# Gate and up products of a two-layer decoder trunk: seven block products in place of eight for the upper half of the input, one core

## The reference, cut to what matters

```python
D_MODEL = 1024
D_FF = 2816
...
def rmsnorm(x, g):
    xf = x.astype(jnp.float32)
    y = xf * lax.rsqrt(jnp.mean(xf * xf, axis=-1, keepdims=True) + EPS)
    return (y * g.astype(jnp.float32)).astype(x.dtype)

def swiglu(x, wi, wo):
    g, u = jnp.split(x @ wi, 2, axis=-1)
    return (jax.nn.silu(g) * u) @ wo

def ffn_half(x, g_pre, g_post, wi, wo):
    return x + 0.5 * rmsnorm(swiglu(rmsnorm(x, g_pre), wi, wo), g_post)
```

## Time and profile before

| | |
|---|---|
| runs | 2091.39 us median of 3 (2090.8 to 2091.59) |
| profiled execution, span from first to last instruction | 2089.9 us |
| PE busy | 2068.6 us, 99% |
| DVE busy | 1125.9 us, 54% |
| ACT busy | 702.9 us, 34% |
| POOL busy | 47.7 us, 2% |
| mean traffic | 97 GB/s |

### The profile page before, as it was taken

One profiled execution on the slowest core, in us unless ns is written; L12 is line 12 of the kernel. 1 busy time (PEld: TensorE's weight loads), 2 busy tenths in 40 slices (PEclk: granted clock), 3 DMA queues, 4 the chain that ended last, 5 costly groups with the idle time before them and its releaser, 6 DMA issues.

```text
span 2089.9 us, 37944 instructions
## 1 busy us (share of the span) xinstructions
PE 2068.6 (99%) x17092; PEld 2046.3 (98%) x17092; DVE 1125.9 (54%) x1509; ACT 702.9 (34%) x877; POOL 47.7 (2%) x95
## 2 busy tenths in 40 slices
PE   8999999999999999999999999999999999999999
PEld 8999999999999999999999999999998999999998
DVE  6443244866768543244686342344898854323467
ACT  5221123423354322122444222122487432212243
POOL 0000000022200000000000000000000000000000
PEclk9999999999999999999999999999999999999999
DMA  5222222145321322222222222222222222222222
GB/s 175 90 90 89 96 102 81 62 153 162 127 108 61 122 81 92 91 102 92 101 82 101 82 96 89 99 84 79 86 97 84 82 101 102 89 94 85 98 92 82
DMA packets 35106, 202.79 MB, mean 97 GB/s; under 512 B 5088, under 2 KB 5376, under 8 KB 17024
## 3 DMA queue, kind: packets, MB, share of 16 engines
q1 hardware_dynamic: 29520, 183.87, 25.0%
q0 software_dynamic: 5424, 16.50, 2.5%
HBM read 193.78 MB, written 4.48 MB: 95 GB/s over the span
## 4 chain that ended last, share of the span: by engine, by line
PE 86%; DVE 11%; ACT 2%; issue 1%; DMA 1%; DVEq 0%; ACTq 0%
PE acc L1825 70%; PE acc L1935 10%; DVE w_lo L1120 2%; DVE t L1233 2%; PE acc L1866 1%; DVE x L1240 1%; DVE act_lo L1246 1%; DMA raw<-in_weights 1%; DVE rs_post L1228 1%; PE acc L2015 1%; PE acc L2069 1%; DVE xsum L1255 1%; DVE rs_pre L1228 0%; PE acc L2093 0%; PE acc L2142 0%
## 5 line engine op out<-in xcount | busy, mean ns | idle before, releaser
L1825 PE MATMUL acc<-act_hi,w_hi 128*128 128x260 f32 x3072 | 621.5, 284 | 0.0
L1825 PE MATMUL acc<-act_hi,w_lo 128*128 128x260 f32 x3072 | 617.8, 283 | 0.0
L1825 PE MATMUL acc<-act_lo,w_hi 128*128 128x260 f32 x3072 | 617.4, 282 | 0.0
L1825 PEld LDWEIGHTS acc<-act_hi,w_hi 128*128 128x128 f32 x3072 | 472.4, 188 | 2.7 <-issue 2.0
L1825 PEld LDWEIGHTS acc<-act_hi,w_lo 128*128 128x128 f32 x3072 | 472.6, 188 | 0.4
L1825 PEld LDWEIGHTS acc<-act_lo,w_hi 128*128 128x128 f32 x3072 | 471.8, 188 | 0.5
L723 ACT ACTIVATE w_hi<-raw 128x2048 fp32r<-128x2048 f32 (+3 forms) x179 | 323.0, 1805 | 297.4 <-DMA raw<-in_weights 297.3
L1120 DVE TENSOR_TENSOR w_lo<-raw,w_hi 128x2048 fp32r<-128x2048 f32 (+3 forms) x179 | 386.4, 2158 | 31.7 <-ACT w_hi L723 31.7
L1370 DVE TENSOR_TENSOR gu<-acc,rs_pre 128x520 f32<-128x520 f32 x164 | 114.3, 698 | 441.1 <-PE acc L1825 441.0
L849 ACT ACTIVATE hid_hi<-gu 128x520 fp32r<-128x520 f32 x86 | 55.0, 639 | 476.6 <-DVE gu L1390 476.6
L1825 PE MATMUL acc<-hid_hi,w_hi 128*128 128x260 f32 x1024 | 206.4, 283 | 0.2
(11 more groups left out here) (308 smaller groups left out, 2141.6 us busy)
## 6 DMA issues: line engine op xcount, KB each, us to landing
raw<-in_weights SPq DMA_DIRECT2D x138, 1024.0 KB, 4.8
raw<-in_weights SPq DMA_DIRECT2D x32, 896.0 KB, 4.5
ring<-in_k_pages POOLq DMA_DIRECT2D x16, 256.0 KB, 3.7
raw<-in_weights SPq DMA_DIRECT2D x12, 256.0 KB, 5.3
x<-in_x SPq DMA_DIRECT2D x8, 260.0 KB, 6.5
out_y<-x SPq DMA_DIRECT2D x8, 260.0 KB, 2.1
ckb<-ch_rows POOLq DMA_DIRECT2D x8, 256.0 KB, 4.5
ring<-in_v_pages POOLq DMA_DIRECT2D x8, 256.0 KB, 3.8
```

Source lines behind the costliest of these rows:

```text
L1825: ins = nc.tensor.matmul(a[0:width, half, 0:HALF], w[slot][:, at:at + width], m[:, half * HALF:(half + 1) * HALF], start=first and n == 0, ...
```

## The change

**Block products.** From pair 5 on (6 in sub-layers 2 and 6, `FIRST_SUM`) a pair is computed otherwise. Input chunks 4 to 7, the gate and up columns and the two token halves form a 2 x 2 by 2 x 2 block product, which takes seven block products (`seven`, 6 matmuls each) in place of eight; chunks 0 to 3 stay as they are (`plain`, 12 matmuls each, four times). A pair has 7 x 6 + 4 x 12 = 90 matmuls. 17 pairs of sub-layers 0 and 4 and 16 of 2 and 6 are made so, 66 in all. The results are put together by DVE: four jobs b, a, c, d per pair, drained by 260 and 520 wide additions; `last_sums`, the one that finishes the up tile from job d, stands in DVE's program at the start of the next pair, or, for a phase's last pair, after everything else of that pair.

**Weights.** Such a pair has two loads: `sums` (four pieces of 256 columns, read as runs of 1 KB, in a space of 1792) and `plain` (1024 columns). GpSimd adds three more blocks to a `sums` load after it has landed (`make_sums`: one addition of 512 columns, two of 256, each waiting for the one ahead). ACT and DVE then split 1792 and 1024 columns. The slots are replaced by one arena of 6144 columns. Loads are placed one behind the other; those of up to 2048 columns start at a multiple of 2048, and what doesn't fit starts at 0. SP issues a load when every earlier load that it overlaps has been used (`blockers`): a `sums` load is used after the seventh block product, at matmul 42 of its pair (`sums_used`), a `plain` load when job d is done, at the pair's end.

**Forms of the input.** Since blocks are added, the input must be normalised first: DVE writes y = x * gain * rs_pre, four differences and sums, and their high and low parts (ACT, DVE), and after the last ordinary pair overwrites `act_hi` and `act_lo` with the split of y: 23 DVE and 11 ACT instructions of 520 columns per sub-layer, spread over the four pairs ahead of the first block pair.

**Down product.** It comes in three parts (PHASES): after pairs 6, 13 and 21. The first two load eight units less wide in k and twice as wide in outputs (7 chunks x 2 tiles, 1792 columns, four loads a part); the number of matmuls is unchanged. In the last pair of a phase ACT and DVE split, in place of the next pair's `sums` and `plain`, the first and the second load of the down product (`split(n)`, `split(n + 1)`).

What the second load of each down part overlaps, by these rules:

| sub-layer | part after pair 6 | part after pair 13 | part after pair 21 |
|---|---|---|---|
| 0 | sums6 | sums13 and plain13 | sums21 |
| 2 | sums6 and plain6 | sums13 and plain13 | sums21 |
| 4 | sums6 | sums13 | sums21 and plain21 |
| 6 | sums6 and plain6 | sums13 | sums21 and plain21 |

So six of the twelve can be issued only when the phase's last pair has ended, the other six at matmul 42 of it.

```diff
-HID = (14, FT - 14)
+PHASES = ((0, 7), (7, 14), (14, FT))
...
+FIRST_SUM = lambda s: 6 if s % 4 else 5
...
+    def place(self, name, pieces, span):
+
+        start = -(-self.top // UNIT) * UNIT if span == UNIT else self.top
+        if start + span > ARENA:
+            start = 0
+        self.top = start + span
...
+    def blockers(self, n):
+
+        at, span = self.loads[n][3:5]
+        return [m for m in range(max(0, n - 8), n)
+                if self.loads[m][3] < at + span and at < self.loads[m][3] + self.loads[m][4]]
...
+                before = PLAN.blockers(n)
+                jobs = [last_job[m] for m in before if not is_sums(m)]
+                if jobs:
+                    sp.wait_ge(acc_ready, max(jobs) + 1)
+                sums = [m for m in before if is_sums(m)]
+                if sums:
+                    sp.wait_ge(sums_used, sums_count(max(sums)))
...
+            def make_sums(n):
+
+                wait_raw(pool, n)
+                pairs = lambda ap: ap.rearrange("p (a n) -> p a n", a=2)
+                made = 2 * (sums_count(n) - 1)
+                nc.gpsimd.tensor_tensor(pairs(quad(n, 4, 2)), pairs(quad(n, 1, 2)),
+                                        quad(n, 3).unsqueeze(1).broadcast_to([P, 2, QUAD]), ALU.add)\
+                    .then_inc(some_sums, 1)
+                pool.wait_ge(some_sums, made + 1)
+                nc.gpsimd.tensor_tensor(quad(n, 6), quad(n, 5), quad(n, 1), ALU.add).then_inc(some_sums, 1)
+                pool.wait_ge(some_sums, made + 2)
+                nc.gpsimd.tensor_tensor(quad(n, 3), quad(n, 6), quad(n, 0), ALU.add).then_inc(sums_made, 1)
...
+            def sum_hidden(s, j, previous):
+
+                n = U[f"{s}.sums{j}"] + 2
+                a, b, c = (acc_of(f"{s}.{part}{j}")[:, :, 0:HALF] for part in "abc")
+                g = gu_of(s, j)[:, 0, :]
+                u2, u4, u3, v = sum_halves(s, j)
+                if previous:
+                    last_sums(s, j - 1)
+                if previous:
+                    sum_product(s, j - 1)
+                dve.wait_ge(one_copied, sums_count(n - 2))
+                drains(nc.vector.tensor_tensor(u2, b[:, 1, :], cols(g, 0), ALU.add), f"{s}.b{j}")
...
+                if previous:
+                    sum_low(s, j - 1)
+                dve.wait_ge(dve_order, mark)
+                drains(nc.vector.tensor_tensor(v, a[:, 0, :], u3, ALU.add), f"{s}.a{j}")
+                split_low(n)
+                wait_job(dve, f"{s}.c{j}")
+                nc.vector.tensor_tensor(cols(g, 0), c[:, 0, :], cols(g, 0), ALU.add)
+                drains(nc.vector.tensor_tensor(cols(g, 1), c[:, 1, :], u4, ALU.add), f"{s}.c{j}")
+                split_low(n + 1)
...
+                    last_sums(s, b - 1)
+                    sum_product(s, b - 1)
+                    sum_low(s, b - 1)
...
+                b = claim(J[f"{s}.b{j}"])
+                seven(b[:, 0, 0:HALF], 1, 3, 1, True)
+                seven(b[:, 1, 0:HALF], 6, 2, 4, True).then_inc(acc_ready, 1)
+                a = claim(J[f"{s}.a{j}"])
+                seven(a[:, 0, 0:HALF], 5, 0, 4, True)
+                seven(a[:, 1, 0:HALF], 4, 1, 4, True).then_inc(acc_ready, 1)
+                c = claim(J[f"{s}.c{j}"])
+                seven(c[:, 0, 0:HALF], 0, 4, 5, False)
+                seven(c[:, 1, 0:HALF], 3, 5, 6, False)
+                d = claim(J[f"{s}.d{j}"])
+                seven(d[:, 0, 0:HALF], 2, 6, 7, False).then_inc(sums_used, 1)
+                wait_unit(n + 1)
+                plain(c[:, 0, 0:HALF], 0, 0, None)
+                plain(c[:, 1, 0:HALF], 0, 1, False).then_inc(acc_ready, 1)
+                plain(d[:, 0, 0:HALF], 1, 0, False)
+                plain(d[:, 1, 0:HALF], 1, 1, True).then_inc(acc_ready, 1)
```

More of the change, by code:

```diff
@@ L66 @@
 UNIT = 2048
-SLOTS = 3
+ARENA = 3 * UNIT
+QUAD = 2 * P
+SUMS = 7 * QUAD
+LOADS = 5
+FORMS = 6
 RING = 4
@@ L114, in add_unit @@
     def add_unit(self, name, what):
-        size = what[3] * sum(b - a for a, b in what[4])
-        self.unit[name] = len(self.units)
-        self.units.append((name, self.size, size, what))
-        self.size += P * size
+        self.place(name, [what], UNIT)
+    def place(self, name, pieces, span):
[3 more added lines that the diff above has]
+        self.top = start + span
+        sizes = [what[3] * sum(b - a for a, b in what[4]) for what in pieces]
+        self.unit[name] = len(self.loads)
+        self.loads.append((name, self.size, sum(sizes), start, span, len(pieces)))
+        for what, size in zip(pieces, sizes):
+            self.units.append((name, self.size, size, what))
+            self.size += P * size
+    def blockers(self, n):
+        at, span = self.loads[n][3:5]
+        return [m for m in range(max(0, n - 8), n)
+                if self.loads[m][3] < at + span and at < self.loads[m][3] + self.loads[m][4]]
     def share_accs(self, turned):
@@ L133, in refills @@
         split_at.update(self.early)
-        return {split_at[n]: n for n in range(2, len(self.units))}
+        return {split_at[n]: n for n in range(2, len(self.loads)) if n in split_at}
 def col(i, n=1):
@@ L175, in ffn @@
     def ffn(s, name, layer):
[L176 to L180 removed]
+        w = (name + "_wi", layer)
+        for a, b in PHASES:
+            for j in range(a, b):
+                if j < FIRST_SUM(s):
+                    pl.add_unit(f"{s}.in{j}", (*w, 0, KC, [col(j), col(FT + j)]))
+                else:
+                    pl.place(f"{s}.sums{j}", [(*w, 6, 2, [col(j)]), (*w, 4, 2, [col(j)]),
+                                              (*w, 6, 2, [col(FT + j)]), (*w, 4, 2, [col(FT + j)])], SUMS)
+                    pl.place(f"{s}.plain{j}", [(*w, 0, 4, [col(j), col(FT + j)])], UNIT // 2)
+            j0 = a
+            if a == 0 and s % 4:
                 first_group(s, [f"{s}.in0", f"{s}.in1", f"{s}.in2"])
                 j0 = 3
[L183 removed]
+            for j in range(j0, b):
+                if j >= FIRST_SUM(s):
+                    for part in "bac":
+                        pl.add_job(f"{s}.{part}{j}")
+                    pl.add_job(f"{s}.d{j}")
+                    pl.last_of_sums[f"{s}.plain{j}"] = f"{s}.d{j}"
+                    continue
                 if j == 0:
```

343 lines of the change are left out of this document (257 added, 86 removed).

## The result

The changed kernel takes 2130.55 us (median of four runs, 2126.45 to 2131.25); the kernel before took 2091.10 us in the same session (four runs, 2089.82 to 2091.59). The ratio is 1.0187, with a 95% interval of 1.0173 to 1.0201: slower, as forecast, but by 39.5 us and not by 16.3, and outside the range (its upper end was 2126).

What follows compares the result with a forecast made beforehand. PE, busy 99% of the span, was taken as the bound. -47.3 + 41.6 + 7 + 11.4 + 3.6 = +16.3 on a span of 2089.9, plus 1.5 to the median, gave 2107.7 us; range for 8 in 10: 2091 to 2126.

Steps and rivals of the forecast that it cites:

- the sum for the forms: Around the first block pair: DVE's work on the input's forms makes PE wait 1.8 us in sub-layers 0 and 4; +3.6 us.
- GpSimd's sums: Additions after a sums load: 2.85 us each load, tight chain 10.4 against 10.75 us, so 0 us on the path.
- terms for waits and clock: Everything added to the saved matmuls: +41.6 and +7 at phase ends, +11.4 for low clock, +3.6 for the forms.
- Matmuls and spacing: All 66 block pairs: 396 fewer matmuls at an unchanged 0.1194 us each, -47.3 us.
- The fourth rival: Block pairs: 6 to 12 matmuls in a row to one bank change the spacing; 2137 or 2078 us, chance 0.06.
- The late second load: Down phases' ends: its split delays the last hid_lo; +41.6 us in six phases, +7 us in the other six.
- The third rival: Phase ends: the chain to the last hid_lo is covered and the saved matmuls remain; 2047.7 us, chance 0.07.
- The clock: Behind the six long waits at phase ends: low clock costs 1.9 us each, +11.4 us; none behind 1.2 us waits.
- The first rival: Phase ends: the gaps come but the clock stays, so 11.4 us fall away; 2096.3 us, chance 0.10.
- with hops this is 12, past the 11.46 us of the pair: Pair ahead of the first block pair: DVE's drain, split, hidden tile and ten form instructions take 12 us.
- in 2 and 6 the wait falls inside the larger one: Sub-layers 2 and 6: the next unit is a down load, so the forms' wait there adds nothing.
- the rival: Block pairs: GpSimd's additions and DVE's two-input instructions hold each other up; ten cases cost 13 us, 2121 us, chance 0.14.

Runs made afterwards that it cites:

- the late split: Changed kernel, but in a phase's last pair ACT and DVE split the second down load behind the last hidden tile: 2068.91 us.
- the split ahead of the silu: Changed kernel, but in the three ordinary pairs ahead of the first block pair ACT splits the next weights before its silu: 2122.24 us.
- the memsets: Changed kernel, but GpSimd writes zeros in place of its three additions per sums load: 2114.54 us.
- the three parts alone: Changed kernel without block products: all pairs ordinary, the down product in three parts and the loads' new places kept: 2099.35 us.
- the filled waits: Changed kernel, but PE does 48 matmuls with overwritten results at each of the six long waits: 2112.76 us.
- both edits: Changed kernel with the second down split behind the last hidden tile and the weights' split before the silu: 2053.40 us; with memsets besides, 2042.09.

## Why the prediction was wrong

The sign and the main mechanism were right, and the forecast was 22.9 us short. Two steps failed, about equally: the sum for the forms (3.6 us), which left out DVE's waits inside it, and GpSimd's sums, put at nothing. The experiments show it by differences. With the late split, the split ahead of the silu and the memsets the time is 2042.1 us; the forecast without its terms for waits and clock is 2089.9 - 47.3 + 1.5 = 2044.1. Of the 88.5 us between that kernel and the change, the late split took 61.6, where the forecast had 41.6 + 7 + 11.4 = 60.0; the split ahead of the silu 15.5, against 3.6; the memsets 11.3, against 0. The shares of the last two depend on the order: alone they took 8.3 and 16.0.

Term by term, from the trace (span 2129.5, forecast 2106.2):

- **Matmuls and spacing: right.** 16696 matmuls, and inside block pairs 42 in 5.01 us and 48 in 5.73, 0.119 each. The fourth rival (one bank for many matmuls in a row) falls.
- **The late second load: right.** Six of 6.0 to 7.0 (39.6 us, forecast 41.6) and six of 1.2 to 1.4 (7.4, forecast 7). Undone and doubled on the chip, both with the forecast's sizes. Undoing it took away 61.6 us: 47.0 listed, 13.1 of clock and the 3.1 of the next point, against which the waits for `w_lo` of the block pairs grew by 2.7. The third rival (the gaps are covered) falls with the twelve waits. What the prediction did not see is that the order could be turned at no cost.
- **A wait costs more than its entry: missed.** 0.26 us each, as measured at the eight places of the three parts alone. For the twelve 3.1 us, for 18 others 4.7.
- **The clock: right in kind, a little small.** 12.5 us (13.1 less the six 0.10) against 11.4; and two waits of 2.1 us had their own stretch, 3.0 us together, against which the one before at 523 us is gone, 1.5. The prediction priced all waits of 1 to 2 us without it, on the one row of 2.2 us behind which none stood. The first rival (the clock stays) falls with the filled waits.
- **The forms: the first step that failed.** Forecast 3.6 us (0 to 8), in sub-layers 0 and 4; measured 10.0 us in nine waits, in all four, and with these waits' own cost (2.3) and the low clock behind one of them (1.4) near 14. The step "with hops this is 12, past the 11.46 us of the pair" added DVE's own instructions and left out that DVE waits inside: 1.69 us for ACT's split behind a silu behind a drain that `stream` delayed. They stand inside the first block pair and not behind it. And "in 2 and 6 the wait falls inside the larger one" was false for them: they are ahead of job d, which releases the late load, so they push the long wait back instead of being covered by it. Only the 0.7 us for `w_lo` behind job d were covered; the long waits there last 6.0 us and not 6.9.
- **GpSimd: the second step that failed, forecast 0; the rival was right in part.** The size of the additions was right (2.8 us alone). But with DVE beside it they take 3.8 and slow DVE. 4.2 us of waits for `w_lo` stand in the list and in no term; they are not all GpSimd's, since with memsets alone 2.8 us of such waits are left, and they are gone only with both edits besides. A share of the forms' waits is GpSimd's too. With memsets 16.0 us go, with both edits 11.3: close to the 13 that the rival had over the forecast. It had a chance of 0.14, with no row for or against; the rule that it quotes should have moved that number, and in the working the splits and products that DVE does beside GpSimd could be counted.
- **A landing: not forecast.** A 1 MB load in sub-layer 5, halved by ACT, landed in 6.9 us and not 4.8, and PE waited 2.1 us with low clock behind it. Its wait differed from run to run (ACT waited 0.3 us for it before, 0.5 to 3.0 in the others, with no order by edit). Its cause stays open.

-1.6 (the twelve waits) + 7.8 (a wait's own cost) + 2.6 (clock: 1.1 + 3.0 - 1.5) + 6.4 (forms) + 4.2 (`w_lo`) + 2.1 (landing) = 21.5 of the 23.3 us; 1.8 us are in no entry.

Several of the small terms were put at nothing, one by one: GpSimd's sums, a landing, a wait's own cost, the clock behind waits of 1 to 2 us. Nothing is the floor of each of them, so an error could only add. Their sum should have stood above zero, and the range higher.

## What to carry to other kernels

Ask of each instruction in an in-order engine what stands behind it and whether that needs it: a split of a load that is 8 us away stood ahead of the one result that PE waited for, and moving it turned a loss of 39 us into a gain of 22. Price a wait of PE as its entry in the list plus 0.26 us here, and another 1.5 to 2.9 if it lasts 3 us or more, since the clock behind it was then low for a while every time. Before an addition goes to the idle GpSimd, look at what DVE does in the same microseconds: here DVE made the same sums in 1.54 us, while GpSimd took 3.8 and slowed DVE.

## What the runs showed of the hardware

- In the thirteen traces the granted clock was at the lower level (1.2 GHz) for a stretch behind each of the 35 waits of PE of 3.0 to 7.9 us inside the run, behind 16 of the 36 of 1.8 to 2.5 us, and behind none of the 57 of 1.15 to 1.66 us. Among those of about 2.2 us the same place (`act_hi` in sub-layer 5) has it in some runs and not in others. Behind the long ones it cost 1.5 to 2.9 us, 0.45 us for each us of the stretch that fell on PE's work; the cost did not grow with the wait.
- A GpSimd addition of 512 columns took 1.29 us alone and up to 3.4 beside DVE instructions with two SBUF operands, and a DVE product took 1.79 us instead of 0.69 beside it. A memset of 512 columns on GpSimd took 0.53 us and slowed nothing that the means show.
- Four runs of the version with both edits lie between 2051.15 and 2060.17 us; with memsets for GpSimd's additions they lie within 1.3 us. Additions that meet DVE at one time or another may be the reason; nothing here shows that.
